# Index scores on 64-row halves between pieces of the query products, key and query copies on ScalarE, three selection rounds moved into the recurrence, gated-linear products on 64-row halves

## What is computed

```python
u = rms_norm(x, norm1_w) @ w_in            # rnn_x, rnn_gate, q, k, v, iq, ik, iw, g
# recurrence
xc = causal_depthwise_conv(rnn_x, ...)
y_rnn = rg_lru(xc, ...) * gelu(rnn_gate)
# index scores, selection, attention
q, k, ik = rms_norm of each head of 64
rel   = relu(einsum('bqhd,bsd->bqhs', iq, ik))      # 8 index heads of 64, one key head
score = einsum('bqhs,bqh->bqs', rel, iw) * idx_scale
_, idx = top_k(score, 128)                          # then attention over those keys alone
```

```python
att  = where(causal, q_dec @ k_inv^T, 0)            # in a chunk
kv_n = k_to_end^T @ v                               # a state update per chunk
S_n  = decay * S_(n-1) + kv_n
o    = att @ v + q_dec @ S_prev
```

## Time and profile before

| | us |
|---|---|
| median of three runs (1658.3 to 1659.3) | 1659.05 |
| the profiled execution | 1657.61 |
| its span | 1655.8 |
| TensorE busy in the span | 1616.1 (98%) |
| VectorE busy | 718.6 (43%) |
| ScalarE busy | 675.3 (41%) |
| GpSimd busy | 794.9 (48%) |
| chain that ended last: PE, DVE, ACT | 89%, 6%, 3% |

### The profile page before, as it was taken

The page is one execution under the profiler, slowest core; times in us unless marked ns, Lnnn a source line. Parts: engine busy times, 40 slices in busy tenths (PEclk is TensorE's granted clock), DMA queues, the critical chain, the costliest instruction groups (busy, mean ns, idle before and its releaser), DMA issues.

```text
span 1655.8 us, 22591 instructions
## 1 busy us (share of the span) xinstructions
PE 1616.1 (98%) x7638; PEld 1318.0 (80%) x7638; DVE 718.6 (43%) x1357; ACT 675.3 (41%) x1088; POOL 794.9 (48%) x1060
## 2 busy tenths in 40 slices
PE   7999998999999999999999998899999999999997
PEld 5787776777888888888888887788978888888885
DVE  5497995664233212121232543634223552452354
ACT  5324775544334323232333424643554442342342
POOL 5244573323555455555454531055744555565553
PEclk9999999999999999999999999999999999999998
DMA  5222221123232332323232321033423233233231
GB/s 189 79 77 77 77 89 64 51 64 113 91 101 90 101 100 91 102 89 101 89 111 89 96 70 52 14 115 101 127 77 100 79 102 105 92 96 103 89 101 64
DMA packets 45060, 149.76 MB, mean 90 GB/s; under 512 B 4600, under 2 KB 7808, under 8 KB 44992
## 3 DMA queue, kind: packets, MB, share of 16 engines
q1 hardware_dynamic: 38016, 138.43, 26.3%
q10 hardware_dynamic: 6976, 10.41, 1.8%
HBM read 146.58 MB, written 2.11 MB: 90 GB/s over the span
## 4 chain that ended last, share of the span: by engine, by line
PE 89%; DVE 6%; ACT 3%; issue 1%; ACTq 0%; DVEq 0%
PE job L320 26%; PE job L322 26%; PE job L321 26%; DVE arena L1373 2%; PE o L497 1%; DVE arena L1376 1%; PE score L399 1%; PE job L763 1%; DVE arena L1810 1%; PE score L435 1%; PE turn L361 1%; ACT w_hi L843 1%; PE score L729 1%; PE turn L462 1%; DVE arena L1519 1%
## 5 line engine op out<-in xcount | busy, mean ns | idle before, releaser
L291 POOL TENSOR_TENSOR w_lo<-w_raw,w_hi 128x256 fp32r<-128x256 f32 x1056 | 794.7, 785 | 835.1 <-ACT w_hi L843 834.5
L320 PE MATMUL job<-a_hi,w_hi 128*128 128x512 f32 (+1 forms) x1120 | 431.3, 385 | 10.0 <-POOL w_lo L291 9.8
L322 PE MATMUL job<-a_hi,w_lo 128*128 128x512 f32 (+1 forms) x1120 | 423.1, 378 | 0.0
L321 PE MATMUL job<-a_lo,w_hi 128*128 128x512 f32 (+1 forms) x1120 | 423.1, 378 | 0.0
L843 ACT ACTIVATE w_hi<-w_raw 128x1024 fp32r<-128x1024 f32 x264 | 275.5, 1052 | 286.0 <-PE job L322 276.2
L320 PE MATMUL job<-b_hi,w_hi 128*128 128x512 f32 x952 | 375.5, 394 | 4.8 <-DVE b_lo L1376 4.8
L322 PE MATMUL job<-b_hi,w_lo 128*128 128x512 f32 x952 | 371.3, 390 | 0.0
L321 PE MATMUL job<-b_lo,w_hi 128*128 128x512 f32 x952 | 371.0, 390 | 0.0
L320 PEld LDWEIGHTS job<-a_hi,w_hi 128*128 128x128 f32 x1120 | 211.1, 188 | 55.3 <-DVE a_lo L1373 10.9
L321 PEld LDWEIGHTS job<-a_lo,w_hi 128*128 128x128 f32 x1120 | 211.2, 189 | 39.4 <-issue 1.9
L322 PEld LDWEIGHTS job<-a_hi,w_lo 128*128 128x128 f32 x1120 | 211.1, 188 | 39.6
(11 more groups left out here) (257 smaller groups left out, 1294.1 us busy)
## 6 DMA issues: line engine op xcount, KB each, us to landing
w_raw<-w_all SPq DMA_DIRECT2D x264, 512.0 KB, 3.5
arena<-x_t ACTq DMA_DIRECT2D x8, 512.0 KB, 6.2
out_t<-arena ACTq DMA_DIRECT2D x8, 256.0 KB, 2.2
arena<-rg_w ACTq DMA_DIRECT2D x1, 1024.0 KB, 5.6
arena<-row_table ACTq DMA_DIRECT2D x1, 1024.0 KB, 5.1
arena<-mem_t ACTq DMA_DIRECT2D x1, 1024.0 KB, 6.6
arena<-consts ACTq DMA_DIRECT2D x1, 384.0 KB, 4.2
cst<-consts ACTq DMA_DIRECT2D x1, 260.0 KB, 7.4
```

Source lines behind the costliest of these rows:

```text
L291: nc.gpsimd.tensor_tensor(w_lo[:, sl, c], raw[:, sl, c], w_hi[:, sl, c].bitcast(F32), ALU.subtract).then_inc(s("lo_ready"), 1)
L320: mm(ps[:, 0:n], w_hi[:, sl, c], hi[:, kt, 0:n], start=kt == 0, stop=False)
L321: mm(ps[:, 0:n], w_hi[:, sl, c], lo[:, kt, 0:n], start=False, stop=False)
L322: ins = mm(ps[:, 0:n], w_lo[:, sl, c], hi[:, kt, 0:n], start=False, stop=kt == last)
```

## The change

- **Start:** TensorE runs J_IQ+1 before `norm_sum(0)`, and `norm_job` goes with J_IQ+2. VectorE's parameter work stands after the first takes. ScalarE's `split(4)` stands ahead of the norm's root, and three small instructions make `q_eps` and `k_eps`.
- **Index scores:** `ikz` becomes `ik`, one tile with the key in both halves and no zeros. A pair of matmuls, one for each head of a tile, runs on rows 0 to 63 and 64 to 127 into two banks. Two pairs stand ahead of J_Q, seven between the slices of J_Q and three between those of J_Q+1. `rel` has four buffers.
- **Keys and queries:** ScalarE copies J_K, J_K+1 and the eight J_Q jobs out of PSUM without the norm's scale; the roots take `k_eps` and `q_eps` for it, one instruction for each token tile. TensorE's query sums stand one job later, and it waits for the key norm before it spreads the second one in the same bank.
- **Selection:** 13 rounds stand in one row on VectorE, and one more round in each of the passes i = 0, 1, 2 of the recurrence. `keep` and `rq` are made at the end of pass 2.
- **Gated-linear mixer:** `g_qd` has two tiles without zeros. Products and state outputs run in pairs on row halves; the state updates make only the 64 output rows that are used, by turns of head and chunk.
- **End:** the sum over the first seven tiles' squares and over the last one are accumulated by TensorE; VectorE multiplies by the spread scale straight from PSUM; SyncE's queue issues four of the eight output DMAs.

TensorE's program after J_K+1, before: all index matmuls, then J_Q.

The diff, cut to its core:

```diff
@@ TensorE
             job(J_IQ, a_hi, a_lo)
+            job(J_IQ + 1, a_hi, a_lo)
             pe.wait_ge(s("const_landed"), 16)
             norm_sum(0)
-            norm_job(1, J_IQ + 1, a_hi, a_lo)
-            job(J_IQ + 2, a_hi, a_lo)
+            norm_job(1, J_IQ + 2, a_hi, a_lo)
...
+            def idx_pair(m):
+                t, i = 1 + m // 4, m % 4
+                if m >= 2:
+                    pe.wait_ge(s("idx_relu"), 2 * m - 2)
+                for h in range(2):
+                    r = slice(64 * h, 64 * h + 64)
+                    mm(idx_banks[m % 2][h][:, 0:P * (t + 1)], p1[r, J_IQ + i, t * P:t * P + P],
+                       ik[r, 0:P * (t + 1)], start=True, stop=True).then_inc(s("idx_mm"), 1)
+            def idx_job(k, pairs):
+                open_job(k)
+                for kt in range(8):
+                    ins = block_of(k, [kt], a_hi, a_lo, pieces=True)
+                    if kt < len(pairs):
+                        idx_pair(pairs[kt])
+                ins.then_inc(s("job_done"), 1)
...
+            idx_pair(0)
+            idx_pair(1)
+            idx_job(J_Q, range(2, 9))
...
+                if k < 2:
+                    pe.wait_ge(s("qk_inv"), 2)
+                    if k == 1:
+                        pe.wait_ge(s("k_normed"), 1)
+                    spread(t_ps[0], 4 + 2 * k, rows=slice(0, 64))
+                    spread(t_ps[0], 5 + 2 * k, rows=slice(64, 128)).then_inc(s("qk_spread"), 1)
+                if k >= 1:
+                    q_sums(k - 1)
             job(J_RNN + 1, a_hi, a_lo)
+            q_sums(7)
             pe.wait_ge(s("qk_root"), 3)
...
-                r = slice(64 * (n % 2), 64 * (n % 2) + 64)
                 for h in range(4):
-                    ins = mm(t_ps[n % 2][:, h * P:h * P + P], g_ke[r, n // 2, h // 2 * P:h // 2 * P + P],
-                             g_vt[h][r, n // 2, :], start=True, stop=True)
+                    out_r = slice(64 * (h % 2), 64 * (h % 2) + 64)
+                    for n in (2 * m, 2 * m + 1)[0:1 if m == 3 else 2]:
+                        r = slice(64 * (n % 2), 64 * (n % 2) + 64)
+                        ins = mm(t_ps[n % 2][out_r, h * P:h * P + P], g_ke[r, m, h * 64:h * 64 + 64],
+                                 g_vt[h][r, m, :], start=True, stop=True)
...
                 for n in range(1, 8):
-                    ins = mm(ps[:, 64 * n:64 * n + 64], g_st[:, h // 2, n, :], g_qd[:, h, 64 * n:64 * n + 64],
-                             start=False, stop=n == 7, skip_group_check=True)
+                    for half in range(2):
+                        r = slice(64 * half, 64 * half + 64)
+                        c = slice(64 * n, 64 * n + 64)
+                        ins = mm((o_ps, s_ps[1])[half][:, c], g_st[r, c2, n, :], g_qd[r, c2, c],
+                                 start=False, stop=n == 7, skip_group_check=True)
@@ ScalarE
+            def act_take(k, dst):
+                act.wait_ge(s("job_done"), k + 1)
+                fn(dst, job_ps[k % 2][:], ACT.Copy).then_inc(s("job_taken"), 1)
@@ VectorE
+            for n in range(TOP_K // 8 - 3):
+                top_round()
+                if n in (1, 3):
+                    key_norm(n // 2)
...
                 gelu_inner(f + 1)
+                if i < 3:
+                    top_round()
                 dve.wait_ge(s("conv_done"), f + 2)
...
-            norm_inverse(7)
+            dve.wait_ge(s("norm_root"), 7)
+            v.reciprocal(rcol[:, :, 0], rcol[:, :, 0]).then_inc(s("norm_inv"), 1)
+            dve.wait_ge(s("norm_spread"), 7)
             for f in range(8):
-                stt(o_out[:, f, :], x[:, f, :], vcol("final", f), rstd[:]).then_inc(s("out_ready"), 1)
+                stt(o_out[:, f, :], x[:, f, :], vcol("final", f), t_ps[0][:]).then_inc(s("out_ready"), 1)
```

More of the change, by code:

```diff
@@ L931, in _, with idx_relu @@
[L931 to L934 removed]
+            def idx_relu(m):
+                t = 1 + m // 4
+                for n in (2 * m, 2 * m + 1):
+                    act.wait_ge(s("idx_mm"), n + 1)
+                    if n >= 4:
+                        act.wait_ge(s("idx_acc"), n - 3)
+                    fn(rel[:, n % 4, 0:P * (t + 1)], idx_banks[m % 2][n % 2][:, 0:P * (t + 1)],
+                       ACT.Relu).then_inc(s("idx_relu"), 1)
@@ new lines, in _ @@
+            for m in range(12):
+                idx_relu(m)
+                if m in (5, 10):
+                    split(J_Q + 3 + m // 6)
+                if m == 8:
+                    act.wait_ge(s("qk_sum"), 2)
+                    act.wait_ge(s("eps_step"), 3)
+                    for t in range(QT):
+                        ins = fn(rcol[:, t, 4:8], sums[:, t, 16:20], ACT.Sqrt, scale=1.0 / 64, bias=k_eps[:, t:t + 1])
+                    ins.then_inc(s("qk_root"), 1)
+                if m == 10:
+                    act_take(J_Q, q_raw[:, 0, :])
@@ L936, in scol @@
+            q_square(0)
+            split(J_Q + 5)
+            for c in range(1, 8):
+                act_take(J_Q + c, q_raw[:, c, :])
+                q_square(c)
+                split(J_Q + 5 + c)
+            act.wait_ge(s("qk_sum"), 10)
+            for t in range(QT):
+                ins = fn(rq[:, t, :], sums[:, t, 0:16], ACT.Sqrt, bias=q_eps[:, t:t + 1])
+            ins.then_inc(s("qk_root"), 1)
+            for k in range(J_Q + 13, J_RNN + 5):
+                split(k)
             def scol(c0, f):
```

256 lines of the change are left out of this document (126 added, 130 removed).

## The result

The changed kernel takes 1648.32 us (median of four, 1647.54 to 1649.87) against 1658.67 for the kernel before in the same session (1657.79 to 1659.30): ratio 0.9939, 95% interval 0.9922 to 0.9956. It is 10.3 us faster where 6.1 were forecast, and inside the range. The profiled execution has a span of 1648.1, 7.7 less than before. It is the slowest of the four and the profile before was a fast one, so the traces show less of the gain than the medians do.

The account below looks back on a forecast made before the run. TensorE, busy for 1616 of 1656 us, was taken to bound the kernel, with VectorE nearly full in the recurrence. Terms -2.9 - 4.0 + 1.5 + 6.3 - 6.2 - 0.8 = -6.1 gave a median of 1653.0 us, range 1646 to 1659.5.

Parts of the forecast that it names:

- Start: Kernel start: TensorE's 2.17 us wait and probably the half clock go, J_K starts at about 44.5: -2.9 us.
- The new wait: At the start, before the index key's sum: TensorE waits about 1.0 us.
- Index: Index scores: 12 half-row pairs between job pieces take 12.5 us instead of 16.5: -4.0 us.
- Keys and queries: Before the recurrence: TensorE waits for query roots (1.1) and two split spreads (0.4), otherwise not for VectorE: +1.5 us.
- Recurrence: Recurrence passes: VectorE's added rounds, `keep` and `rq` delay TensorE, plus 0.5 of half clock: +6.3 us, between +1.1 and +8.
- the half clock: Recurrence pass 3, behind TensorE's stop: a half-clock stretch costing 0.5 us, between 0 and 1.9.
- The stop: Pass 3 of the recurrence: TensorE stands some 4.6 us before job k+4; idle for 3 to 6 us as the sign.
- Mixer: Gated-linear mixer: row-half pairs save 1.5 on products, 2.2 on state updates, 2.5 on state outputs: -6.2 us.
- the rival that halves don't pay: Mixer: pairs of few columns may be bound by weight loads, so products and outputs give nothing: 1658 us, chance 0.15.
- End: Kernel end: scale copy and its step go (-0.65), two DMA queues (-0.15), split square sum 0: -0.8 us.
- The slower one: Recurrence: VectorE's own instructions stretch beside GpSimd, adding +12 and losing all the rest at +6: 1665 us, chance 0.1.
- TensorE bounds the recurrence too: Recurrence: VectorE's pauses hold the rounds and `keep`, so +6.3 falls to about +1: 1647.5 us, chance 0.2.

Follow-up runs that it names:

- i_block: Changed kernel with the half-row index pairs in two blocks ahead of J_Q and J_Q+1 instead of between the jobs' pieces: 1648.25 us.
- e_copy: Changed kernel with ScalarE's copy of the last scale to SBUF back, so the last products read it from there: 1648.17 us.
- v_14: Changed kernel with 14 selection rounds ahead of the recurrence, two in passes 0 and 1 and none in pass 2: 1647.42 us.
- m_old: Changed kernel with the gated-linear mixer as in the kernel before (whole rows, zero-padded queries): 1656.21 us.
- m_serial: Changed kernel with the mixer's same half-row matmuls one head or row half after the other instead of by turns: 1654.21 us.
- e_add: Changed kernel with the last square added by VectorE again and one plain norm sum at the end: 1648.14 us.
- v_front: Changed kernel with no extra VectorE work in passes 1 and 2; rounds ahead of them, `keep` and `rq` in pass 0: 1644.53 us.
- s_old: Changed kernel with the norm's sum before J_IQ+1 again: 1651.34 us.
- v_none: Changed kernel without the three selection rounds in passes 0 to 2 (that computation is missing), `keep` and `rq` left: 1645.46 us.

## Why the prediction was right, point by point

**Start:** right. No wait, no half clock, J_K at 43.98 (44 to 45). The new wait was 0.3 to 0.5 and not 1.0, so the term is -3.5 and not -2.9.

**Index:** right in size (-4.2 for -4.0), and for the right reason, the overlap of the halves. The pairs cost 0.84, 1.06 and 1.27, to 0.01 what I carried over from the earlier trace rows (from the start of the last matmul ahead of a pair to the start of the second behind it, less two steps of 0.227: 58.24 to 59.53 for 256 columns). What i_block adds is that the last us of this term is not worth anything, as TensorE waits for the first key norm behind it.

**Keys and queries:** mis-sized, +2.7 for +1.5. The wait for the roots (0.9 against 1.1) was there. Missed was the wait for the first key norm before the second key's spread, 1.1: I had said that TensorE waits for nothing of VectorE, but both spreads now use one bank, and VectorE's norm of the first key stands behind its second round.

**Recurrence:** the mechanism and its place (before job k+4 of pass 3) were right, four sizes were off, in both directions, and that the sum came near is in part luck. Forecast and measured are: what pass 1 adds 1.1 and 1.2; the round of pass 2 1.5 and 1.3; `keep` and `rq` 3.2 and 1.6; lateness that TensorE bears, nothing and 0.6; the half clock 0.5 and 1.6. The stop was 2.7 in place of 4.6, just under the 3 to 6 that I had named as its sign. `keep` and `rq` were 1.57 and not 3.2, because I took 2.02 for the three large instructions from the earlier trace rows without a look at who works beside them. GpSimd did, in the kernel before, and `keep` began at 146.09:

```profile
144.06 3.50 POOL L291 TENSOR_TENSOR w_lo<-w_raw,w_hi 128x256 fp32r<-128x256 f32 x4 [1.02 <-ACT w_hi L843]
```

In the changed kernel they stand in GpSimd's pause of 9.5 us and take 0.89. The half clock cost 1.6, near the worst of my 0 to 1.9; by e_copy's trace it costs nothing in other executions, so 0 to 1.6 is what the runs show. For pass 2 I counted 1.74 of waiting as room for the round, and the same there. v_14 shows that such room is used once only: the waits in a pass are for ScalarE, which itself waits for VectorE, so a late VectorE doesn't catch up on them.

**Mixer:** mis-sized, -8.3 for -6.2 up to job 18. The products gave 1.2 (1.5 forecast) and the outputs 2.5, as forecast, but by my own terms the outputs should have given 6.0 less 3.1 less 0.8, which is 2.1. The trace has about 0.3 of switching a stretch, 0.6 in all, where I had 0.8, so the hit is partly luck. The state updates gave 3.6: a group of 16 takes 0.67 in place of 1.71, the last 8 take 0.65 in place of 1.16. My own terms give 3.1 to 4.7 for them (three groups at 0.86 or 0.43, and 0.58 for the last 8), and the "1.8 to 3.1, take 2.2" that I wrote does not follow from them; this is the term that was mis-sized.

The remaining 0.9 is a square sum that moved behind job 18, and 0.7 of it does come back there, as I had expected. From job 18's first matmul to the first turn of the sliding-window attention is 24.1 in the changed kernel and 23.4 in the kernel before and in m_old. It doesn't show in the sliding-window stage as a whole, which from job 18 to the last products is 56.8 long in both, because each has a stretch of 3.4 us at clock 0.50 in it: by m_old's trace, which has none and takes 55.5, it costs 1.2 in the kernel before and 0.6 in the changed one. So the mixer is worth 8.3 at job 18 and about 7.6 behind it.

**The rule on weight loads.** The outputs' rows stepped by 0.11 per pair, so the rival that halves don't pay fell. The Trainium skill, "TensorE: Matmul & The Clock Gate", section "Step-by-step: what each phase is for", says that the load's time goes by columns and not by rows. m_serial agrees with it (a half-row matmul alone follows the one before by about 0.11, as whole rows do), and the conclusion that I had drawn as a rival was still wrong, since the rule is on one load and not on two matmuls that use different rows.

**End:** -0.8 forecast, 0.0 in the trace; e_add shows which half failed. I had the split sum as 0, which it is at full clock. In the traces at half clock its spread begins up to 0.9 later, and that eats the copy's 0.6.

**Rivals.** The slower one didn't come. Over its own passes 1 and 2 (172.55 to 199.18 and 199.18 to 225.86) VectorE is busy for 25.90 and 25.95 where it was for 22.51 and 22.98 (177.57 to 202.98 and 202.98 to 228.40). That is 3.4 and 3.0 more for a round of 3.2, so nothing was stretched. "TensorE bounds the recurrence too" was wrong for this kernel, and holds for v_front.

What stays open. The wait for the last low part, ahead of the `b_hi` job, is 4.7 to 4.8 in most traces and 3.7 in those of m_old, s_old and m_serial, whose code is the same there. In the changed kernel two pairs of inputs of pass 3 take 1.81 and 1.83, in those three 1.28; but v_none, v_14 and e_copy have 1.29 and still wait for 4.7, since their TensorE arrives earlier. What stretches those inputs is not shown. Nor is the gain put down to parts beyond the traces' 7.8: the 2.5 that the medians have on top lie within what executions of these kernels differ by.

## What to carry to other kernels

When work is moved to where an engine "has time", look at what its waits are for. A wait for a partner that is itself fed by this engine isn't room: work put there lengthens the loop by nearly its whole cost in every later pass, while a wait for an engine that runs on its own is free. Here the same three rounds and `keep` cost nothing in waits of the second kind, ahead of the passes and in pass 0, and in passes 1 and 2 they cost 3.4 us of TensorE's time, with 1.6 of half clock behind it in some executions.

Look behind a gain for the next wait: what the index pairs save by standing inside the jobs (1.0 us) TensorE waits off at the next spread.

## What the runs showed of the hardware

A half-row matmul alone follows the one before by about 0.11 us, as a whole-row one does (11 in 1.44, 14 in 1.67), but two on different row halves start within 10 ns of each other. On 64 by 64 tiles 16 matmuls took 0.67, four starting within 0.03 us of each other; on 64 by 128 tiles with shared rows 16 took 1.71. Two on the same 64 rows that differ in columns only started within 10 ns too (the last 8 of a group in 0.65). How much of this comes from the weight load of 64 columns in place of 128, and how much from the overlap, no run separates.

A pair of half-row matmuls between two pieces of a job, with the switch to half rows and back, adds 0.84, 1.06 and 1.27 us for 256, 384 and 512 columns.

A stop of TensorE of 2.7 us was followed by 3.4 us at clock 0.50 in the changed kernel, which cost 1.6, and by clock 1.00 in e_copy, whose code is the same there. Stops of 0.75 and 1.45 at the same place (v_none, v_14) were followed by 1.00. In m_serial the clock was 0.50 from 1003 to 1006, in job 18, without any stop, behind 56 narrow half-row matmuls that ran for the most part one after the other; in the changed kernel, where they ran two at a time, it was 1.00 there. That their order is the cause isn't shown.
